# Hyena filter sum moved to ScalarE by tile and GpSimd, weight splits and value turns moved earlier in a two-layer encoder

## What is computed

```python
def hyena_mixer(u, ...):                       # u: normed stream, (T, D)
    p = conv_centred(u @ w_in + b_in, conv_w, conv_b)   # (T, 3 D), taps -1, 0, 1
    x0, x1, v = p[..., :D], p[..., D:2*D], p[..., 2*D:]
    v = v * x1
    k = hyena_filters(T, ...)                  # (2T-1, D), k / sum(|k|, axis=0)
    y = irfft(rfft(v, 2*T) * rfft(k, 2*T))[:T]
    y = (y + v * skip) * x0
    return y @ w_out + b_out

def hyena_filters(T, ...):
    h = (sine MLP of the positions) @ w4       # (T, 2 D): forward and backward half
    h = h * decay
    hf, hb = h[:, :D], h[:, D:]
    k = concatenate([hf, 0, hb[:0:-1]])
    return k / sum(abs(k), axis=0)
```

## Time and profile before

| | us |
|---|---|
| three runs | 1658.91, 1655.14, 1669.92 |
| their median | 1658.91 |
| the profiled execution, its own time | 1657.11 |
| its span (first to last instruction) | 1655.3 |
| mean granted TensorE clock | 0.978 of full |

### The profile page before, as it was taken

How to read it: one execution, slowest core, us unless ns; L and a number is a source line. 1 busy time by engine, 2 the same in 40 slices (tenths; PEclk the granted TensorE clock), 3 DMA queues, 4 the chain that set the end, 5 groups by cost and what they waited for, 6 DMA issues and landing times.

```text
span 1655.3 us, 22040 instructions
## 1 busy us (share of the span) xinstructions
PE 1609.3 (97%) x8334; PEld 1348.0 (81%) x8334; DVE 1244.3 (75%) x1186; ACT 975.9 (59%) x884; POOL 70.7 (4%) x84
## 2 busy tenths in 40 slices
PE   8998999999999998999999999999999999999996
PEld 7765699999599587888888888888888888888885
DVE  5488556654657545988888888888898888888883
ACT  3374344432446125776777776777677777777762
POOL 0160000000103300000000000000000000000000
PEclk9999999999989997999999999999999999999997
DMA  9331255565135044999999999999999999999990
GB/s 279 102 102 52 61 163 168 172 208 171 49 104 175 26 153 172 372 370 335 364 370 335 361 371 333 364 368 334 362 371 334 357 375 334 362 369 334 363 357 26
DMA packets 221125, 429.58 MB, mean 260 GB/s; under 512 B 9514, under 2 KB 76592, under 8 KB 220752
## 3 DMA queue, kind: packets, MB, share of 16 engines
q1 hardware_dynamic: 217816, 424.82, 72.7%
q10 hardware_dynamic: 3256, 4.06, 0.8%
HBM read 427.80 MB, written 1.05 MB: 259 GB/s over the span
## 4 chain that ended last, share of the span: by engine, by line
PE 90%; DVE 6%; ACT 2%; issue 1%; DMA 1%; ACTq 0%; DVEq 0%
PE ps L1603 87%; PE ps L1615 3%; DVE arena L1021 1%; DVE ring_lo L1223 0%; ACT arena L613 0%; DVE arena L1124 0%; DMA raw<-in_moe_w_gate_dram 0%; DVE arena L1135 0%; DVE arena L1129 0%; DVE arena L1136 0%; DVE arena L1157 0%; DMA ktab<-in_k_table_dram 0%; DVE arena L1125 0%; DVE arena L1130 0%; DVE arena L1106 0%
## 5 line engine op out<-in xcount | busy, mean ns | idle before, releaser
L1391 DVE TENSOR_TENSOR w_lo<-raw,w_hi 128x2048 fp32r<-128x2048 f32 x224 | 511.8, 2290 | 77.7 <-ACT w_hi L912 76.8
L912 ACT ACTIVATE w_hi<-raw 128x2048 fp32r<-128x2048 f32 x224 | 428.9, 1919 | 179.5 <-DMA raw<-in_moe_w_gate_dram 92.4
L1603 PE MATMUL ps<-w_hi,xg_hi 128*128 128x512 f32 x904 | 358.1, 396 | 5.0 <-DVE w_lo L1571 2.1
L1603 PE MATMUL ps<-w_hi,xg_lo 128*128 128x512 f32 x904 | 353.4, 391 | 0.0
L1603 PE MATMUL ps<-w_lo,xg_hi 128*128 128x512 f32 x904 | 352.7, 390 | 0.0
L1395 DVE TENSOR_TENSOR w_lo<-raw,w_hi 128x2048 fp32r<-128x2048 f32 x110 | 251.6, 2287 | 44.9 <-ACT w_hi L916 44.7
L916 ACT ACTIVATE w_hi<-raw 128x2048 fp32r<-128x2048 f32 x110 | 211.1, 1919 | 78.4 <-DMA raw<-in_moe_w_down_dram 76.9
L1603 PEld LDWEIGHTS ps<-w_hi,xg_hi 128*128 128x128 f32 x904 | 170.2, 188 | 39.9 <-DVE w_lo L1571 2.5
L1603 PEld LDWEIGHTS ps<-w_hi,xg_lo 128*128 128x128 f32 x904 | 170.0, 188 | 36.3
L1603 PEld LDWEIGHTS ps<-w_lo,xg_hi 128*128 128x128 f32 x904 | 170.3, 188 | 33.9
L1603 PE MATMUL ps<-w_hi,eh_hi 128*128 128x512 f32 x440 | 173.9, 395 | 4.8 <-issue 4.8
(11 more groups left out here) (284 smaller groups left out, 1908.0 us busy)
## 6 DMA issues: line engine op xcount, KB each, us to landing
raw<-in_moe_w_gate_dram SPq DMA_DIRECT2D x112, 1024.0 KB, 5.1
raw<-in_moe_w_up_dram SPq DMA_DIRECT2D x112, 1024.0 KB, 5.3
raw<-in_moe_w_down_dram SPq DMA_DIRECT2D x112, 1024.0 KB, 5.0
ring<-in_w_in_ab_dram SPq DMA_DIRECT2D x12, 1024.0 KB, 6.5
ring<-in_hy_w_in_dram SPq DMA_DIRECT2D x12, 1024.0 KB, 5.1
ring<-in_ffn_w_gate_dram SPq DMA_DIRECT2D x11, 1024.0 KB, 5.3
ring<-in_ffn_w_up_dram SPq DMA_DIRECT2D x11, 1024.0 KB, 5.4
ring<-in_ffn_w_down_dram SPq DMA_DIRECT2D x8, 1408.0 KB, 6.8
```

The source lines that it names most:

```text
L912: nc.scalar.activation(w_hi[:, j, :], raw[:, j, :], ACT.Copy).then_inc(sem("gu_high"), 1)
L1391: V.tensor_tensor(w_lo[:, j, :], raw[:, j, :], w_hi[:, j, :].bitcast(F32), ALU.subtract).then_inc(sem("gu_split"), 1)
L1603: return nc.tensor.matmul(o, l, r, start=start, stop=stop)
```

## The change

It touches five things. The absolute values are taken by token tile, in the order 0, 2, 1, and ahead of `norm_high(0)`. The sums of the halves go from VectorE to GpSimd, after the KO subtractions, one for each token tile, so `kabs_sum` counts to 3. The high half of block 46 is made before the `kspec` copies, its low half right behind the normalisation; the zeroing of `pad` and the low half of block 47 come before the inversion of `kn`. The two slots of `ring_hi2` are exchanged for blocks from 46 on (`high_of`). The six turns `vx` are put into the third round of the projection, three after its second block and three after its third, with the copies on ScalarE after first taps 3 and 5; the third round is written out behind a loop of two. `vtok` moves to `xn` and `sq`, away from `ring_hi2`.

```diff
-    add("hy", 0, 24)
-    add("vx", 0, 6)
+    add("hy", 0, 20)
+    add("vx", 0, 3)
+    add("hy", 20, 2)
+    add("vx", 3, 3)
+    add("hy", 22, 2)
...
-        vtok = area(14864, 3, D)
+        vtok = [xn[:].rearrange("p k t -> p (k t)")[:, D * i:D * i + D] for i in range(2)] + [sq[:].rearrange("p k t -> p (k t)")[:, 0:D]]
...
+        def high_of(n, k):
+            return ring_hi[:, n % 2, 0:256 * k] if n < B_HY else ring_hi2[:, (n + 1) % 2, 0:256 * k]
...
+            for i, (lt, n) in enumerate(((0, P), (2, META), (1, P))):
+                pool.wait_ge(sem("kabs_ready"), i + 1)
+                g(nc.gpsimd.tensor_tensor(kfb[0:n, lt, 0:D], kfb[0:n, lt, 0:D], kfb[0:n, lt, D:2 * D], ALU.add), sem("kabs_sum"))
...
+            for lt, n in ((0, P), (2, META), (1, P)):
+                act.wait_ge(sem("kt_scaled"), 1 if lt == 0 else 3)
+                act.wait_ge(sem("ke_ready"), 1 if lt == 0 else 2)
+                act.wait_ge(sem("ko_ready"), 1 if lt == 0 else 2)
+                a(nc.scalar.activation(kfb[0:n, lt, :], kfb[0:n, lt, :], ACT.Abs), sem("kabs_ready"))
             norm_high(0)
-            act.wait_ge(sem("kt_scaled"), 3)
...
-            a(nc.scalar.activation(kfb[:, 0:2, :], kfb[:, 0:2, :], ACT.Abs), sem("kabs_ready"))
-            a(nc.scalar.activation(kfb[0:META, 2, :], kfb[0:META, 2, :], ACT.Abs), sem("kabs_ready"))
+            ring_high(B_HY)
             for k in range(8):
...
-            ring_high(B_HY)
             ring_high(B_HY + 1)
...
-            for k in range(6):
...
+                if b in (3, 5):
+
+                    half = b // 2 - 1
+                    for tt, (t0, n) in enumerate(TOKS):
+                        copy("vx", 3 * half + tt, vtok[tt][0:n, 512 * half:512 * half + 512], n, slice(0, 512))
...
             split_norm(C_NMO, "xn3_ready")
-            dve.wait_ge(sem("ko_ready"), 2)
-            for i, (pp, ts) in enumerate(((P, slice(0, 2)), (META, slice(2, 3)))):
-                dve.wait_ge(sem("kabs_ready"), i + 1)
-                v(V.tensor_tensor(kfb[0:pp, ts, 0:D], kfb[0:pp, ts, 0:D], kfb[0:pp, ts, D:2 * D], ALU.add), sem("kabs_sum"))
+            ring_low(B_HY)
+            dve.wait_ge(used("kspec"), 8)
+            v(V.memset(pad[:, :, 0:1], 0.0))
+            v(V.memset(pad[:, :, T + 1:T + 2], 0.0), sem("pad_zero"))
+            ring_low(B_HY + 1)
             t = ready(dve, "kn", 0)
...
+            with pe.Fori(0, 2) as i:
+                for b in range(4):
+                    in_columns(i, b)
+            for b in range(4):
+                in_columns(2, b)
+                if b in (1, 2):
+                    pe.wait_ge(sem("v_ready"), 1)
+                    for k, (t0, n) in enumerate(TOKS):
+                        o = open_tile("vx", 3 * (b - 1) + k)
+                        for c in range(4):
+                            last = turn(o[0:n, P * c:P * c + P], hyc[:, 8 + 4 * (b - 1) + c, t0:t0 + n])
                         close(last)
...
-            pe.wait_ge(used("vx"), 6)
             for k in range(8):
                 half, f = k // 4, slice(P * (k // 2 % 2), P * (k // 2 % 2) + P)
+                pe.wait_ge(used("vx"), 3 * half + 3)
```

More of the change, by code:

```diff
@@ L903, in _ @@
                     ring_high(B_HY + b // 2 + 2, 2)
-            for k in range(6):
-                tt, half = k // 2, k % 2
-                n = TOKS[tt][1]
-                copy("vx", k, vtok[0:n, tt, 512 * half:512 * half + 512], n, slice(0, 512))
+                if b in (3, 5):
+                    half = b // 2 - 1
+                    for tt, (t0, n) in enumerate(TOKS):
+                        copy("vx", 3 * half + tt, vtok[tt][0:n, 512 * half:512 * half + 512], n, slice(0, 512))
             def high_gu(j, S):
@@ L1221, in ring_low @@
                 c = slice(0, 256 * k)
-                high = (ring_hi if n < B_HY else ring_hi2)[:, n % 2, c]
+                high = high_of(n, k)
                 V.tensor_tensor(ring_lo[:, n % RING, c], ring[:, n % RING, c], high.bitcast(F32), ALU.subtract).then_inc(sem("ring_split"), 1)
@@ L1349, in taps @@
                 mult_add(o, pad[:, b, 2:2 + T], w2, o, sem("taps_ready"))
-            ring_low(B_HY)
-            ring_low(B_HY + 1)
             with dve.Fori(0, 2) as i:
@@ L1943, in _, with in_columns @@
                 pe.wait_ge(used(g), j + 1)
-            with pe.Fori(0, 3) as i:
-                for b in range(4):
-                    n = B_HY + b
-                    pe.wait_ge(sem("ring_split"), n - B_FF + 1 + 4 * i)
-                    w_hi_, w_lo_ = split_block(n)
-                    for j in range(2):
+            def in_columns(i, b):
+                n = B_HY + b
+                pe.wait_ge(sem("ring_split"), n - B_FF + 1 + 4 * i)
+                w_hi_, w_lo_ = split_block(n)
+                for j in range(2):
+                    if isinstance(i, int):
+                        o = open_tile("hy", 8 * i + 2 * b + j)
+                    else:
@@ L1950, in _ @@
                         pe.wait_ge(used("hy"), 8 * i + 2 * b + j + 1)
                         o = ps[(base_hy + 2 * b + j) % 8]
-                        for k in range(KT):
-                            m = slice(P * j, P * j + P)
-                            last = product(o[:, 0:T], w_hi_[:, k, m], w_lo_[:, k, m], (xn_hi[:, k, :], xn_lo[:, k, :]), k == 0, k == KT - 1)
-                        close(last)
-            pe.wait_ge(sem("v_ready"), 1)
-            for k in range(6):
-                t0, n = TOKS[k // 2]
-                o = open_tile("vx", k)
-                for c in range(4):
-                    last = turn(o[0:n, P * c:P * c + P], hyc[:, 8 + 4 * (k % 2) + c, t0:t0 + n])
-                close(last)
@@ L1964, in _ @@
-            pe.wait_ge(used("vx"), 6)
+                    for k in range(KT):
+                        m = slice(P * j, P * j + P)
+                        last = product(o[:, 0:T], w_hi_[:, k, m], w_lo_[:, k, m], (xn_hi[:, k, :], xn_lo[:, k, :]), k == 0, k == KT - 1)
+                    close(last)
+            with pe.Fori(0, 2) as i:
[9 more added lines that the diff above has]
+                            last = turn(o[0:n, P * c:P * c + P], hyc[:, 8 + 4 * (b - 1) + c, t0:t0 + n])
+                        close(last)
@@ L1965, in _ @@
             for k in range(8):
                 half, f = k // 4, slice(P * (k // 2 % 2), P * (k // 2 % 2) + P)
+                pe.wait_ge(used("vx"), 3 * half + 3)
                 o = open_tile("vspec", k)
                 for tt, (t0, n) in enumerate(TOKS):
-                    last = mm(o[:, :], (CF, SF)[k % 2][0:n, tt, f], vtok[0:n, tt, 512 * half:512 * half + 512], tt == 0, tt == 2)
+                    last = mm(o[:, :], (CF, SF)[k % 2][0:n, tt, f], vtok[tt][0:n, 512 * half:512 * half + 512], tt == 0, tt == 2)
```

15 lines of the change are left out of this document (5 added, 10 removed).

## The result

The changed kernel takes 1647.85 us (median of 20 runs, 1643.41 to 1657.37), the kernel before 1660.78 us beside it (20 runs, 1654.31 to 1671.66). The ratio is 0.9923, with a 95% interval of 0.9908 to 0.9937: 12.9 us faster, between 10.5 and 15.3. That is inside the range, and under 1% as forecast, but it is twice the 6.2 us of the sum. The forecast time, 1652, lay 4 us above the median. So the range was hit in part by luck, and what remained was to find the other half.

What follows compares the result with a forecast made beforehand. TensorE, at 90% of the chain, was taken to bound the kernel. Terms of 0.82 + 2.6 (3.4 us up to the projection) and 2.85 gave 6.2 us, 1652 for a median; range 1644 to 1661.

Steps and rivals of the forecast that it cites:

- The wait for the sums: Between the filter's transform and `kn`: TensorE's 0.82 us wait for VectorE's sums goes entirely, with GpSimd's sums done by 441.5.
- The splits: Between `kn` and the projection: TensorE's idle time falls from 3.48 to 0.9 us, gain 2.6, bounds 2.25 and 2.8.
- The third round: Around the projection's third round: waits of 2.41 and 0.44 us go, gain 2.85 us, bounds 2.4 and 2.85.
- The port: GpSimd's sums beside VectorE's normalisation: one collision, up to 3.2 us on VectorE, held by 3.7 us of cover at cost 0.
- Rival A: Two collisions at the port, 6.4 us on VectorE: gain only 3.7 us, 1655; chance 15%.
- The clock: At `kn` and the projection's first blocks: a 2.6 us loss left as is; bounds gain 2.6, loss 1.7.
- Rival B: Clock back at once in the projection's first blocks: 2.6 us more, gain 8.8, 1650; chance 12%.
- What is won before 543 us should arrive at the end one for one.: From `vspec` to the end: everything hangs on TensorE's progress, so earlier gains should reach the end in full.
- the written-out third round: In the projection: writing the third round out instead of looping costs nothing, as other straight blocks run at the same pace.
- The range: Whole kernel: 1644 to 1661 us should hold 8 in 10, with some 5 us of median scatter around each case.
- a gain over 1%: Whole kernel: needs 16.6 us, more than the edits' idle time (6.7 us) and the clock's 2.6 together; 6%, for scatter.
- Rival D: In the experts' stage: the edits work but that stage, near the pace of memory, hides the gain, 1658; chance 8%.

Runs made afterwards that it cites:

- unroll_only: Kernel before with the third round written out and `vtok` in `xn` and `sq`, turns still behind the round, filter part undone: 1656.16 us, 0.9975.
- turns_only: Kernel before with only the turns moved into the written-out third round and `vtok` in `xn` and `sq`, filter part undone: 1652.74 us, 0.9951.
- before_pad1: Kernel before plus one matmul of one column, result unread, in the stop ahead of `vspec`: 1654.72 us, 0.9963.
- changed_pad1: Changed kernel plus one matmul of one column at the start of `vspec`: 1650.11 us, 0.9926 against the kernel before.
- front_only: Kernel before with only the filter's part (absolute values by tile, sums on GpSimd, splits beside the transform), loop of three rounds kept: 1654.07 us, 0.9975.
- unroll_old_buffer: Kernel before with the third round written out, turns behind it, `vtok` in its old place in the arena: 1658.62 us, 0.9973.
- Before_pad8: Kernel before plus eight matmuls of one column, results unread, in the stop ahead of `vspec`: 1656.91 us, 0.9987.

## Why the prediction was right, and where it was not

**The wait for the sums, 0.82 us.** Right: `kn` starts straight behind the transform. The sums took 2.34 to 2.43 us on GpSimd, not the 3.21 that I took from the subtraction; three took 7.1 us, below my lower bound of 8.2. The subtraction's row holds a collision of its own, I think: VectorE's 128x1024 addition runs from 436.00 to 437.22 in the changed kernel, the subtraction from 436.23 to 439.44, which is 2.22 us from the addition's end. That is argued; no run separates the two. 16 rows took as long as 128.

**The splits, 2.6 us.** Right: 3.48 became 0.82 us, a gain of 2.66.

**The third round, 2.85 us.** Right: both waits are gone, no `v_ready`, and the bursts take 1.31 us against 1.4. unroll_only and turns_only differ only in where the turns stand, and by 125.3 - 122.0 = 3.3 us.

**The port.** Right in kind and in cost, wrong in count. I had one collision that the 3.7 us of cover holds, and Rival A had two at 6.4 us. Two came, with the second and the third sum, and cost 2.7 us together: the first instruction met its sum 0.8 us before the end and lost 0.6 us; the second met nearly a whole one and lost 2.1, since a sum takes 2.4 us and not 3.2. In four further profiles with the sums on GpSimd the pair took 3.24 to 4.01 us. So it stayed under the cover, partly by luck. The Trainium skill's rule (SBUF — State Buffer, § Who interferes with whom) had the second and the third sum stop the split of the stream, and the trace agrees, for the `SCALAR_TENSOR_TENSOR` with two SBUF inputs: 1.10 and 2.58 us against 0.50 each.

**The clock.** I left it out with bounds of 2.6 better and 1.7 worse. Transform and `kn` were 2.0 us longer and the first blocks 1.3 shorter in one execution, and transform and `kn` 0.8 shorter in the other, with first blocks of 15.01 us. The sum of it is 0.7 us to either side, inside the bounds; but the transform's part, up to 1.25 us longer, I had not counted at all. Rival B, the whole 2.6 at once, did not occur (13.58 and 15.01 us, not 12.33).

**"What is won before 543 us should arrive at the end one for one."** This is the step that failed, and with it the unwritten term in the sum: that code which is not edited keeps its time. The gain did arrive, but some 5 us came with it from 1,070 us later, where TensorE's stop fell from 4.78 to 1.71 us and the half clock behind it went. I had costed the written-out third round at nothing, because its blocks run at the same pace. They do; but a round that is written out, and turns that stand elsewhere, shift all of TensorE's code behind them, and where it lies decides the stop. The row was there to be read, in section 5 of the page of before, and again in that of the change:

```profile
L1603 PE MATMUL ps<-w_hi,eh_hi 128*128 128x512 f32 x440 | 173.9, 395 | 4.8 <-issue 4.8
```

```profile
L1612 PE MATMUL ps<-w_hi,eh_hi 128*128 128x512 f32 x440 | 172.8, 393 | 1.7 <-issue 1.7
```

All idle time of 440 matmuls is one stop, with nothing named that ends it. It is the largest "issue" piece of the whole chain, and I had read the chain only for the stage of the edits.

**The range.** 1644 to 1661 held it, thanks to the scatter that I put around the cases, and in so far by luck: none of the cases held the gain at the exit. The 6.7 us of idle time that I set against a gain over 1% left out the 0.44 us; with it they are 7.15, which changes no chance. Rival D did not occur either: the experts' stage hid nothing.

**What stays open.** That the placement of code decides is shown by before_pad1: one instruction without work, the stop 1.58 instead of 4.78 or 5.26, the stage alike, and a ratio under 1. That the long stop is a wait for a second block of code is read from TensorE's rows and the packets, in fourteen profiles; no kernel was made that brings the long stop back (changed_pad1 might have, and did not). Open is what sets the clock's phase: why it fell behind a stop of 2.41 us in front_only, unroll_only and unroll_old_buffer, and not in the two profiles of the kernel before nor, behind 2.29, in before_pad1; why layer 0 has its two lengths, and why the transform is slower in most kernels with the third round written out. Before_pad8's small gain is open too; its profile has the whole gain at the exit and a slow layer 0.

## What to carry to other kernels

Read the whole chain for "issue" pieces before you sum up a change: a stop of several us with no releaser behind a jump may be a fetch of code, to be seen as a packet of kind "instruction" in the DMA view and as a long row of the jump in the engine's sequencer, and any edit of that engine's program can take it away, here 5 us of 1660. When a result is larger or smaller than its stalls, compare period by period, and run a control that changes the code and not the work; one matmul of one column was enough here. And when two edits free the same path, try the simpler alone: here the order did it, whichever engine summed.

## What was not expected of the hardware

- The jump over the unused body took TensorE 4.40 to 4.76 us in fourteen profiles, its other jumps in the kernel before 0.08 to 0.24. Seen in the matmuls it was a stop of 1.6 to 2.0 us in eleven programs and of 4.8 and 5.3 in one, with one or two packets of code ahead; from packet to next matmul it was 2.6 to 2.7 us each time.
- The granted clock behind a stop. Behind 4.78 and 5.26 us it was 0.50 and 0.70. Behind 1.6 to 2.0 us it was full, except once at 0.66. Behind 2.3 to 2.4 us it was full in three profiles and 0.60 to 0.62 in three, and behind 2.64 it was 0.50.
- GpSimd's addition of 128x1024 in 2.35 us, against 3.21 for the subtraction of the same shape, and the same time for 16 rows.
